# Block 1's attention: probabilities scaled before a transposition by the identity, and the gate product of branch 2 taken out of the eighth head

## The chip, the cores and the metric

The kernel runs on one core of one Trainium2 chip. The metric is the device time of one execution in microseconds (us); the kernel before took 2315.72 us, the median of 3 runs (2314.38 to 2320.10).

## What is computed

Two transformer blocks on 512 tokens of width 1024, in fp32. The first has two branches that read the same normalised input `h`: softmax attention (8 query heads, 2 key/value heads, head size 128) and a bidirectional gated delta rule (8 heads, chunks of 64). Each is gated per head, projected, gated again by a sigmoid of a product with `h`, and added. The change touches the attention of this block and the gate of the second branch:

```python
def block(qi):                                   # 128 queries of one head, 512 keys
    s = jnp.einsum('bkgqd,bksd->bkgqs', qi, k).astype(jnp.float32) * scale
    pr = jax.nn.softmax(s, axis=-1).astype(v.dtype)
    return jnp.einsum('bkgqs,bksd->bkgqd', pr, v)
...
y_att = (o_att * jax.nn.silu(az)) @ w_br_att[i]
y_dn = (o_dn * jax.nn.silu(dz)) @ w_br_dn[i]
mix = (jax.nn.sigmoid(gate_att) * y_att + jax.nn.sigmoid(gate_dn) * y_dn) @ w_out[i]
```

The second block (two layers: stick-breaking attention and differential attention, each with a SwiGLU feed-forward part) is not touched.

## The kernel before

**Matrix products.** Activations are feature-major, 8 tiles of 128 features by 512 tokens. Every large product is made in three matmuls of rounded halves: high weights by high input, high weights by low input, low weights by high input. The weights come as a stream of 1 MB loads (`raw<-wstream`, L1478), each with 16 blocks of 128x128; ACT rounds them to the high half (`w_hi`, L2442), DVE subtracts to get the low half (`w_lo`, L1989). In the profile such matmuls are `ps<-hh,spl` and `ps<-hl,spl` (moving operand first, then the weights). `gemm(op, K, done)` makes one output tile of 128 features: 8 blocks, 24 matmuls, in one of two PSUM banks; `done` starts what evicts it.

**The order** is made before the program is written. `arrange` walks through the large products on PE, and beside them keeps lanes, each a generator of the steps of one side chain: `att_lane` for a head's attention, `conv_lane`, `prep_lane` and `scan_lane` for the delta rule, `silu_lane` and `early_lane` for gates. Between matmuls a lane is advanced when its costs say that its engines are free (`Order.step`, `PRIORITY`, costs in us in `cost=[...]`), or by force when the main stream needs what it holds (`until`). Every engine then runs its own steps in the order of this one list and waits for semaphores; nothing is reordered on the chip. So a changed cost of one step moves others on all engines.

**A head** (loop over `hd`, L695 on) is five large products (convolution inputs k, q and v, attention's query, attention's gate `az`), and from the second head on two more: `dz` of the head before (the delta rule's output gate) and a gate product of branch 2, `early_done(hd - 1)`. `EARLY = 7` says how many of the eight gate products of branch 2 are made among the heads. Such a product is turned into a sigmoid in three steps on ACT (`eg_sig`, tile `X[7]`), stored to HBM by SP (`eg_out`, L1491, printed as `spill<-x`) and loaded again (`eg_ld`, L1498) before the branches are added. After the heads come the eight gate products of branch 1 and the one left of branch 2, and then the products of the attention branch (`ps<-arena_r,spl`). Their operand is what the heads stored: SP loads it tile by tile (`re_ld`, L1526) after the normalised output of the last head (`on_b`, PE `ps<-on_t,cst`, stored at L1516) is out, ACT rounds it, DVE makes its low half (`re_lo`, L2220).

**Attention of one head** is four blocks of 128 queries. `at_s` is the scores (PE, one fp32 matmul 128x512), its row maximum (DVE, L2072) and the exponential with the row sum (ACT, L2439, tile `att_p` in `x`). `at_n` on DVE takes the reciprocal of the sum (L2078) and makes a diagonal matrix of it (L2080). `at_t` multiplies each 128x128 piece of the unnormalised probabilities by the diagonal on PE (`ps<-diag,x`), which transposes and scales at once, and ACT evicts the result (L2442, `x<-ps`). `at_o` is the product with the values (`ps<-x,arena`).

```python
ts(diag[:, :], C["ident"], ri[:, i:i + 1], None, ALU.mult)          # at_n, L2080
i = mm(psum[u.b][:, c], att_p[:, c], diag[:, :], kb == 0, kb == 3)  # at_t, L1655
def tr(out, in_):                                                   # L1551
    return pe.transpose(out, in_, C["ident"])
```

All matmuls are recorded at L1549 (`mm`) and all transpositions but one at L1552 (`tr`). `tr` is used already for the keys and values of the delta rule (`tr_k`, `tr_v`: `ps<-cst,arena` and `ps<-cst,x`).

Of the kernel before, what the change touches and what calls it, by code (L numbers as in the profile page):

```python
# [10 lines left out]
ALU = mybir.AluOpType  # L11
# [4 lines left out]
KT = 8  # L16
EPS = 1e-6
FFN_HALF = 11
EARLY = 7
LAM_INIT = 0.8 - 0.6 * math.exp(-0.3)  # L20
MAGIC = 12582912.0
TWO_PI = 2.0 * math.pi
# [208 lines left out]
def arrange(o, n_pairs):  # L231
# [41 lines left out]
    def gemm(op, K, done):  # L273

        o.until(main.ready)
        u = main.take()
        ks = range(K) if isinstance(K, int) else K
        for k in ks:
            block(u, op, k, k == ks[0], k == ks[-1])
            if k != ks[-1]:  # L280
                o.step()
        done(u)
        o.step()
# [144 lines left out]
    def att_lane(hd):  # L428
        while ("ar_out", f"q{hd}") not in o.at:
            yield  # L430
        o.behind(o.at["ar_out", f"q{hd}"])
        iq, uo = o.at["ar_out", f"q{hd}"].iq, None
        for qb in range(5):
            hint = "AC DV PE"
            yield hint
            while not ring.ready((qb > 0) + (qb < 4)):
                yield hint
            if qb > 1:
                while not uo and not obank_att.ready():
                    yield hint  # L440
                uo = uo or obank_att.take()
                o.behind(o.at["at_t", hd, qb - 2])
                o.add("at_o", hd, qb - 2, cost=[("PE", 0.9)], u=uo)
            t = max(o.now, o.at["at_n", hd, qb - 1].t) if qb else o.now
            if qb:
                banked("at_t", hd, qb - 1, cost=[("PE", 0.45), ("AC", AC_B)])
                o.now = t
            if qb < 4:
                banked("at_s", hd, qb, cost=[("PE", PE_B), ("DV", DV_B), ("AC", AC_B)]).iq = iq
                yield "DV"  # L450
                o.add("at_n", hd, qb, cost=[("DV", 0.15), ("DV", 0.2)])
        o.behind(o.at["at_t", hd, 3])
        yield "PE"
        o.add("at_o", hd, 3, cost=[("PE", 0.9)], u=uo)
        yield "DV"
        q_slots.give(iq, o.at["at_s", hd, 3])
        while ("az_out", hd) not in o.at:
            yield "DV"
        o.behind(o.at["az_out", hd])
        st = o.add("at_m", hd, cost=[("DV", DV_B)])  # L460
        st.u, st.i = uo, o.at["az_out", hd].i
        ua_outs[st.i] += 1
        st.out_n = ua_outs[st.i]
        obank_att.give(uo)
        ua_slots.give(st.i, st)
# [221 lines left out]
    def early_done(m):  # L687
        def done(u):
            u.t = o.clock["PE"]
            o.spawn("egat", early_lane(m, u))  # L690
        return done

    o.margin = MARGIN_1
    for hd in range(8):
        o.spawn("att", att_lane(hd))  # L695
        o.spawn("prep", prep_lane(hd))
        o.spawn("scan", scan_lane(hd))
        o.until(pads.ready)
        gemm(h, KT, conv_done(8 + hd))
        gemm(h, KT, a_rope(f"q{hd}"))  # L700
        o.until(pads.ready)
        gemm(h, KT, conv_done(hd))
        o.until(ua_slots.ready)
        gemm(h, KT, z_done("az", hd, ua_slots))
        o.until(pads.ready)
        gemm(h, KT, conv_done(16 + hd))
        if hd:
            o.until(lambda: not dz_slots.held[(hd - 1) % 2])
            gemm(h, KT, z_done("dz", hd - 1, dz_slots))
            gemm(h, KT, early_done(hd - 1))  # L710
        if hd == 7:
            o.until(lambda: not dz_slots.held[1])
            gemm(h, KT, z_done("dz", 7, dz_slots))
# [561 lines left out]
def build(nc, wstream, wba, consts, vecs, cossin, pos, xT, pT, outT):  # L1275
# [6 lines left out]
    with ctx:  # L1282
# [20 lines left out]
        pad = sb("pad", [128, 2, S])  # L1303
        small = sb("small", [128, 600])
        GS = sb("GS", [128, 2, S])
        diag = sb("diag", [128, 128])
        ident_r = sb("ident_r", [128, 128], F32R)
        mask_r = sb("mask_r", [128, 130], F32R)
        NA = 41
# [235 lines left out]
        def tensor(pe):  # L1545
# [9 lines left out]
            for q in steps:  # L1555
# [92 lines left out]
                elif kind == "at_t":  # L1648
# [3 lines left out]
                    w.wait_ge(sem("at_p"), at[("at_n",) + q.key].n)  # L1652
                    for kb in range(4):
                        c = slice(kb * 128, kb * 128 + 128)
                        i = mm(psum[u.b][:, c], att_p[:, c], diag[:, :], kb == 0, kb == 3)  # L1655
                    i.then_inc(filled[u.b], 1)
                elif kind == "at_o":
                    (hd, qb), u, g = q.key, q.u, q.key[0] // 4
# [308 lines left out]
        def vector(dve):  # L1967
# [15 lines left out]
            for q in steps:  # L1983
# [90 lines left out]
                elif kind == "at_n":  # L2074
# [2 lines left out]
                    empty(s.u)  # L2077
                    dve.reciprocal(ri[:, i:i + 1], sm[:, i:i + 1]).then_inc(sem("at_rcp"), 1)  # L2078
                    w.wait_ge(sem("at_rcp"), q.n)
                    ts(diag[:, :], C["ident"], ri[:, i:i + 1], None, ALU.mult).then_inc(sem("at_p"), 1)  # L2080
                elif kind in ("az_out", "dz_out"):
                    dst = (ua if kind == "az_out" else dz_of)[q.i]
                    w.wait_ge(sem(kind[:2] + "_sig"), 3 * q.n)
# [843 lines left out]
def lay_out(a):  # L2927

    out = []
    blocks = []  # L2930

    def fm(w, c0, n=1, k0=0, k1=None):
        k1 = w.shape[0] // 128 if k1 is None else k1
        for m in range(n):
            for k in range(k0, k1):
                blocks.append(w[k * 128:k * 128 + 128, c0 + m * 128:c0 + m * 128 + 128])
                if len(blocks) == 16:
                    out.append(np.concatenate(blocks, axis=1))
                    blocks.clear()

    def fm2(w, c0, w1, c1):
        for k in range(8):
            fm(w, c0, 1, k, k + 1)
            fm(w1, c1, 1, k, k + 1)

    def tm(w, c0, n):
        assert not blocks
        for j in range(n):
            out.append(w[:, c0 + j * 256:c0 + j * 256 + 256].reshape(8, 128, 256).transpose(1, 0, 2).reshape(128, 2048))

    w = a["w_in"][0]
    fm2(w, 1024, w, 1152)
    tm(w, 1280, 1)
    for hd in range(8):
        fm(w, 2560 + 1024 + 128 * hd)
        fm(w, 128 * hd)
        fm(w, 2560 + 128 * hd)
        fm(w, 1536 + 128 * hd)
        fm(w, 2560 + 2048 + 128 * hd)
        if hd:  # L2960
            fm(w, 5664 + 128 * (hd - 1))
            fm(w, 7712 + 128 * (hd - 1))
    fm(w, 5664 + 128 * 7)
    fm(w, 6688, 8)
    fm(w, 7712 + 128 * EARLY, 8 - EARLY)
    fm(a["w_br_att"][0], 0, 8)
    fm(a["w_br_dn"][0], 0, 8)
    fm(a["w_out"][0], 0, 8)
    fm(a["w_ple_proj"][0], 0, 8)
    fm2(a["w_ple_gate"][0], 0, a["w_ple_gate"][0], 128)  # L2970
    fm(a["w_ple_gate"][0], 256, 6)
    for i in range(2):
        w = a["w_in_2"][i]
        for m in range(8):
            if m == 0 and i == 0:
                fm2(w, 0, w, 1024)
            else:
                fm(w, 128 * m)
                fm(w, 1024 + 128 * m)
            if m == 0:  # L2980
                tm(w, 2048, 4)
        for k0, k1 in ((0, 4), (4, 8)):
            fm(a["w_out_2"][i], 0, 8, k0, k1)
        for half in range(2):
            for k in range(FFN_HALF * half, FFN_HALF * half + FFN_HALF):
                fm(a["w_gate_2"][i], 128 * k)
                fm(a["w_up_2"][i], 128 * k)
            for m in range(8):
                fm(a["w_down_2"][i], 128 * m, 1, FFN_HALF * half, FFN_HALF * half + FFN_HALF)
    assert not blocks  # L2990
    return np.stack(out)
# [55 lines left out]
```

## Time and profile before

| | |
|---|---|
| median of 3 runs | 2315.72 us |
| the profiled execution | 2313.51 us |
| its span, first to last instruction | 2311.7 us |
| granted clock of TensorE, mean | 0.987 of full speed |
| PE busy | 2215.5 us (96%), 15014 matmuls |
| DVE busy | 1185.2 us (51%), 2101 instructions |
| ACT busy | 1011.8 us (44%), 1919 instructions |
| POOL busy | 248.7 us (11%), 273 instructions |
| DMA | 186.31 MB, mean 81 GB/s |

Busy times of the engines overlap; the share of one engine says how far it could be the bound over the whole span, and a stretch has to be looked at by itself. The heads run from about 85 to 640 us, their last side chains and the gate products to about 732 us. A row with an arrow (`<-`) gives the idle time of the engine ahead of the instruction and what ended it.

### The profile page before, as it was taken

The page shows a single profiled execution, that of the slowest core. Times are in us where ns is not written, and L with a number is a line of the kernel's source. Part 1 is how long each engine was busy: PE and PEld are TensorE (multiplying, and loading weights), DVE is VectorE, ACT ScalarE, POOL GpSimd, SP SyncE. Part 2 cuts the span into 40 slices and gives each one's busy share as a digit, 9 for nine tenths or more (in the row PEclk, how much of TensorE's full clock was granted, in tenths as well). Part 3 has the DMA queues.
Part 4 walks back from the last instruction along what each step waited for, and adds up shares of the span by engine and source line. Part 5 has one row for each costly group of instructions (what it writes and reads, how often), then busy time and mean ns, then how long its engine had stood idle before and what let it go on. Part 6 is the DMA issues. An engine that isn't in the chain of part 4 may idle for free.

```text
span 2311.7 us, 35566 instructions
## 1 busy us (share of the span) xinstructions
PE 2215.5 (96%) x15014; PEld 1709.8 (74%) x15014; DVE 1185.2 (51%) x2101; ACT 1011.8 (44%) x1919; POOL 248.7 (11%) x273
## 2 busy tenths in 40 slices
PE   6999999999999999899999999999999988999999
PEld 4777776777776887686656888888886556888887
DVE  5566666565654455523235643454547665443542
ACT  4565655655555235534454322233435544231331
POOL 0022211221220011002221000001001001000000
PEclk9999999999999999999999999999999989999999
DMA  4222211212213432121102232222221112322222
GB/s 168 74 74 74 70 65 57 84 65 66 74 66 116 153 128 91 56 74 40 52 19 78 91 103 98 91 91 99 84 74 37 37 37 73 104 97 91 91 101 81
DMA packets 35054, 186.31 MB, mean 81 GB/s; under 512 B 4032, under 2 KB 4416, under 8 KB 15696
## 3 DMA queue, kind: packets, MB, share of 16 engines
q1 hardware_dynamic: 34896, 184.05, 23.1%
q8 instruction: 118, 1.93, 0.3%
q14 instruction: 40, 0.33, 0.0%
HBM read 173.26 MB, written 8.16 MB: 78 GB/s over the span
## 4 chain that ended last, share of the span: by engine, by line
PE 86%; DVE 7%; ACT 3%; issue 2%; DMA 1%; POOL 0%; SPq 0%; POOLq 0%; DVEq 0%; ACTq 0%
PE ps L1549 85%; ACT arena L2439 1%; DVE spl L1989 1%; PE ps L1552 1%; DVE x L2316 0%; DVE arena L2139 0%; DVE hl L2284 0%; ACT hh L2439 0%; ACT arena L2442 0%; DMA x<-xT 0%; DVE arena L2178 0%; ACT spl L2442 0%; ACT x L2439 0%; DVE x L2280 0%; DVE x L2264 0%
## 5 line engine op out<-in xcount | busy, mean ns | idle before, releaser
L1549 PE MATMUL ps<-hh,spl 128*128 128x512 f32 x3232 | 1067.2, 404 | 31.5 <-DVE arena_r L2216 7.7
L1549 PEld LDWEIGHTS ps<-hh,spl 128*128 128x128 f32 x3232 | 606.1, 189 | 189.8 <-issue 45.2
L1549 PE MATMUL ps<-hl,spl 128*128 128x512 f32 x1552 | 630.9, 407 | 0.0
L1989 DVE TENSOR_TENSOR spl<-raw,spl 128x512 fp32r<-128x512 f32 x596 | 413.6, 720 | 174.0 <-ACT spl L2442 173.0
L1549 PE MATMUL ps<-arena_r,spl 128*128 128x512 f32 x1936 | 474.9, 401 | 9.1 <-DVE arena_r L2216 4.6
L1549 PEld LDWEIGHTS ps<-arena_r,spl 128*128 128x128 f32 x1936 | 366.6, 190 | 105.3 <-DVE arena_r L2216 5.9
L2442 ACT ACTIVATE spl<-raw 128x512 fp32r<-128x512 f32 x596 | 342.4, 618 | 142.2 <-PE ps L1549 141.1
L1549 PEld LDWEIGHTS ps<-hl,spl 128*128 128x128 f32 x1552 | 293.3, 189 | 73.9 <-issue 18.4
L1549 PE MATMUL ps<-arena 32*32 32x32 f32 (+7 forms) x5664 | 217.5, 225 | 16.7 <-issue 6.1
L2439 ACT ACTIVATE arena<-arena 128x512 f32<-128x512 f32 (+3 forms) x209 | 138.4, 663 | 190.3 <-DVE arena L2321 141.5
L1549 PEld LDWEIGHTS ps<-arena 32*32 32x32 f32 (+4 forms) x5664 | 126.2, 116 | 103.1 <-issue 77.1
L1549 PE MATMUL ps<-arena,cst 128*128 128x512 f32 (+3 forms) x308 | 110.2, 483 | 18.6 <-DVE arena L1996 14.3
L2442 ACT ACTIVATE arena_r<-arena 128x512 fp32r<-128x512 f32 x60 | 37.8, 631 | 201.4 <-DVE arena L2328 191.7
L2439 ACT ACTIVATE arena<-ps,small 128x512 f32<-128x512 f32 (+3 forms) x121 | 68.9, 572 | 128.6 <-PE ps L1549 73.5
L2439 ACT ACTIVATE arena<-ps 128x512 f32<-128x512 f32 (+3 forms) x91 | 60.4, 670 | 143.7 <-PE ps L1549 139.6
L2316 DVE TENSOR_TENSOR x<-x,ps 128x512 f32<-128x512 f32 x64 | 43.8, 684 | 147.0 <-PE ps L1549 147.0
L2864 POOL TENSOR_TENSOR arena<-arena 128x512 f32<-128x512 f32 x30 | 38.9, 1296 | 660.0 <-ACT arena L2439 660.0
L1549 PE MATMUL ps<-spl,hh 128*128 128x256 f32 x576 | 108.7, 290 | 0.0
L1549 PEld LDWEIGHTS ps<-spl,hh 128*128 128x128 f32 x576 | 89.9, 191 | 5.5 <-issue 4.9
L1549 PEld LDWEIGHTS ps<-arena,cst 128*128 128x128 f32 x308 | 53.8, 195 | 41.0 <-issue 24.8
L2325 DVE TENSOR_TENSOR arena<-ps,arena 128x512 f32<-128x512 f32 x44 | 30.4, 691 | 104.4 <-PE ps L1549 104.4
L1549 PE MATMUL ps<-spl,hl 128*128 128x256 f32 x288 | 81.3, 282 | 0.0
(218 smaller groups left out, 1927.6 us busy)
## 6 DMA issues: line engine op xcount, KB each, us to landing
raw<-wstream SPq DMA_DIRECT2D x149, 1024.0 KB, 4.9
GS<-g_rows SPq DMA_DIRECT2D x16, 256.0 KB, 3.5
spill<-x SPq DMA_DIRECT2D x15, 256.0 KB, 2.0
arena<-spill SPq DMA_DIRECT2D x13, 256.0 KB, 5.2
arena<-arena SPq DMA_DIRECT2D x20, 128.0 KB, 2.1
on_t<-spill SPq DMA_DIRECT2D x10, 256.0 KB, 3.2
x<-xT SPq DMA_DIRECT2D x4, 512.0 KB, 7.1
spill<-arena SPq DMA_DIRECT2D x8, 256.0 KB, 2.0
```

What stands on the lines that cost most here:

```text
L1549: return pe.matmul(out, lhsT, rhs, start=start, stop=stop, skip_group_check=True)
L1552: return pe.transpose(out, in_, C["ident"])
L1989: tt(spl[:, p % 2, 1, c], raw[:, p % 2, c], spl[:, p % 2, 0, c].bitcast(F32), ALU.subtract) \
L2316: tt(X[q.m], X[q.m], psum[q.u.b][:, :], ALU.add).then_inc(drained[q.u.b], 1)
L2325: tt(p, psum[q.u.b][:, :], SQ[q.g.name][2], ALU.mult).then_inc(drained[q.u.b], 1)
L2439: return act.activation(out, in_, func, **kw)
L2442: return act.activation(out, in_, ACT.Copy)
L2864: tt(acc, acc, tmp[q.i], ALU.add).then_inc(sem("sq_pool"), 1)
```

## The change

In `at_n` DVE multiplies the tile of probabilities itself (128x512, in place) by the column of reciprocals, where it made the 128x128 diagonal; the tile `diag` is gone. `at_t` is four transpositions by the constant identity, through `tr`. The second cost of `at_n` in the planner is 0.5 where it was 0.2. `EARLY` is 6: the second to the seventh head have a gate product of branch 2 each, the eighth none, and product 6 is made with product 7 after the gate products of branch 1, where its sigmoid goes straight to its tile. The weight stream is laid out in the new order.

```diff
--- before.py
+++ after.py
@@ -16,7 +16,7 @@
 KT = 8
 EPS = 1e-6
 FFN_HALF = 11
-EARLY = 7
+EARLY = 6
 LAM_INIT = 0.8 - 0.6 * math.exp(-0.3)
 MAGIC = 12582912.0
 TWO_PI = 2.0 * math.pi
@@ -448,7 +448,7 @@
             if qb < 4:
                 banked("at_s", hd, qb, cost=[("PE", PE_B), ("DV", DV_B), ("AC", AC_B)]).iq = iq
                 yield "DV"
-                o.add("at_n", hd, qb, cost=[("DV", 0.15), ("DV", 0.2)])
+                o.add("at_n", hd, qb, cost=[("DV", 0.15), ("DV", 0.5)])
         o.behind(o.at["at_t", hd, 3])
         yield "PE"
         o.add("at_o", hd, 3, cost=[("PE", 0.9)], u=uo)
@@ -707,7 +707,8 @@
         if hd:
             o.until(lambda: not dz_slots.held[(hd - 1) % 2])
             gemm(h, KT, z_done("dz", hd - 1, dz_slots))
-            gemm(h, KT, early_done(hd - 1))
+            if hd <= EARLY:
+                gemm(h, KT, early_done(hd - 1))
         if hd == 7:
             o.until(lambda: not dz_slots.held[1])
             gemm(h, KT, z_done("dz", 7, dz_slots))
@@ -1303,7 +1304,6 @@
         pad = sb("pad", [128, 2, S])
         small = sb("small", [128, 600])
         GS = sb("GS", [128, 2, S])
-        diag = sb("diag", [128, 128])
         ident_r = sb("ident_r", [128, 128], F32R)
         mask_r = sb("mask_r", [128, 130], F32R)
         NA = 41
@@ -1652,7 +1652,7 @@
                     w.wait_ge(sem("at_p"), at[("at_n",) + q.key].n)
                     for kb in range(4):
                         c = slice(kb * 128, kb * 128 + 128)
-                        i = mm(psum[u.b][:, c], att_p[:, c], diag[:, :], kb == 0, kb == 3)
+                        i = tr(psum[u.b][:, c], att_p[:, c])
                     i.then_inc(filled[u.b], 1)
                 elif kind == "at_o":
                     (hd, qb), u, g = q.key, q.u, q.key[0] // 4
@@ -2077,7 +2077,7 @@
                     empty(s.u)
                     dve.reciprocal(ri[:, i:i + 1], sm[:, i:i + 1]).then_inc(sem("at_rcp"), 1)
                     w.wait_ge(sem("at_rcp"), q.n)
-                    ts(diag[:, :], C["ident"], ri[:, i:i + 1], None, ALU.mult).then_inc(sem("at_p"), 1)
+                    ts(att_p, att_p, ri[:, i:i + 1], None, ALU.mult).then_inc(sem("at_p"), 1)
                 elif kind in ("az_out", "dz_out"):
                     dst = (ua if kind == "az_out" else dz_of)[q.i]
                     w.wait_ge(sem(kind[:2] + "_sig"), 3 * q.n)
@@ -2959,6 +2959,7 @@
         fm(w, 2560 + 2048 + 128 * hd)
         if hd:
             fm(w, 5664 + 128 * (hd - 1))
+        if 0 < hd <= EARLY:
             fm(w, 7712 + 128 * (hd - 1))
     fm(w, 5664 + 128 * 7)
     fm(w, 6688, 8)
```

The changed costs and the missing product move steps on every engine; the order differs from the first attention head to the start of the attention branch, and on PE not after it.

PE, in the first attention head, from its first scores on (`ps<-arena 128x512` is a block's scores, `ps<-cst,arena` a transposition of the delta rule's keys), before:

```order
L1549 MATMUL ps<-arena 128x512
L1549 MATMUL ps<-hl,spl 128x512
L1549 MATMUL ps<-hh,spl 128x512 x2
L1549 MATMUL ps<-hl,spl 128x512
L1549 MATMUL ps<-hh,spl 128x512 x2
L1549 MATMUL ps<-hl,spl 128x512
L1552 MATMUL ps<-cst,arena 128x128 x4
L1549 MATMUL ps<-hh,spl 128x512 x2
L1549 MATMUL ps<-diag,x 128x128 x4
L1549 MATMUL ps<-arena 128x512
```

and with the change:

```order
L1549 MATMUL ps<-arena 128x512
L1549 MATMUL ps<-hl,spl 128x512
L1549 MATMUL ps<-hh,spl 128x512 x2
L1549 MATMUL ps<-hl,spl 128x512
L1549 MATMUL ps<-hh,spl 128x512 x2
L1549 MATMUL ps<-hl,spl 128x512
L1552 MATMUL ps<-cst,arena 128x128 x4
L1549 MATMUL ps<-hh,spl 128x512 x2
L1552 MATMUL ps<-cst,x 128x128 x4
L1549 MATMUL ps<-arena 128x512
```

The first block stands where it stood, with the transpositions in the place of the products; later ones move by some matmuls to either side.

SP, from the rotation transfer of the eighth head's query (L1487) to the first reloads of the attention branch (`arena<-spill`, `on_t<-spill`, L1526; L1482 stores a head's attention, L1516 its delta rule output), before:

```order
L1487 DMA arena<-arena 64x512
L1478 DMA raw<-wstream 128x2048 x3
L1491 DMA spill<-x 128x512
L1482 DMA spill<-x 128x512
L1478 DMA raw<-wstream 128x2048
L1516 DMA spill<-arena 128x512
L1478 DMA raw<-wstream 128x2048 x3
L1516 DMA spill<-arena 128x512
L1526 DMA arena<-spill 128x512
L1526 DMA on_t<-spill 128x512
L1478 DMA raw<-wstream 128x2048
L1526 DMA on_t<-spill 128x512
```

and with the change:

```order
L1487 DMA arena<-arena 64x512
L1478 DMA raw<-wstream 128x2048 x3
L1482 DMA spill<-x 128x512
L1478 DMA raw<-wstream 128x2048
L1516 DMA spill<-arena 128x512
L1478 DMA raw<-wstream 128x2048 x3
L1516 DMA spill<-arena 128x512
L1526 DMA arena<-spill 128x512
L1478 DMA raw<-wstream 128x2048
L1526 DMA on_t<-spill 128x512 x2
```

The gate product's store (L1491) is gone from the eighth head, and a weight load now stands ahead of the second reload, where it stood ahead of the third. On PE, 45 large matmuls stand between the second matmul row of the last `ps<-on_t,cst` and the first `ps<-arena_r,spl`, where there were 48.

## Rows read from the trace of the kernel before

**Rows 1.** The page: busy time of PE, and the granted clock in 40 slices

```profile
PE 2215.5 (96%) x15014; PEld 1709.8 (74%) x15014; DVE 1185.2 (51%) x2101; ACT 1011.8 (44%) x1919; POOL 248.7 (11%) x273
...
PEclk9999999999999999999999999999999989999999
```

**Rows 2.** Windows: busy us of PE, PEld, DVE, ACT, POOL; clock, DMA share, GB/s

```profile
225.00:640.00 415.00, 399.69 (x5499) 308.25 (x5485) 261.63 (x548) 244.19 (x494) 83.60 (x94) 1.00 0.21 70
sum 650.00, PE 622.36 PEld 481.94 DVE 392.38 ACT 377.25 POOL 128.78; mean PE 207.45 PEld 160.65 DVE 130.79 ACT 125.75 POOL 42.93
...
221.00:226.00 5.00, 4.77 (x74) 3.50 (x75) 4.28 (x9) 3.54 (x8) 1.36 (x2) 0.66 0.13 20
735.00:745.00 10.00, 8.38 (x22) 5.64 (x23) 5.99 (x10) 7.22 (x14) 0.00 (x0) 0.66 0.53 159
```

**Rows 3.** Waits of PE, 85 to 740 us: us in total, times, longest

```profile
PE ps L1549 <- issue: 6.1, 6, 1.5
PE ps L1549 <- DVE arena L2178: 5.1, 7, 1.2
PE ps L1549 <- ACT pad L2442: 3.8, 2, 2.9
PE ps L1549 <- DVE arena_r L2220: 3.0, 2, 2.2
PE ps L1549 <- DVE spl L1989: 2.7, 2, 1.5
```

**Rows 4.** Timeline, first attention block: start, us, engine, line, operation

```profile
87.23 0.69 DVE L2072 TENSOR_REDUCE small<-ps 128x1 f32<-128x512 f32 x1 [2.43 <-PE ps L1549]
...
88.77 0.16 DVE L2078 RECIPROCAL small<-small 128x1 f32<-128x1 f32 x1 [0.25 <-ACT x L2439]
88.97 0.29 DVE L2080 TENSOR_SCALAR diag<-cst,small 128x128 f32<-128x128 f32 x1
...
89.60 1.05 PE L1549 MATMUL ps<-diag,x 128*128 128x128 f32 x8
...
90.49 1.02 PE L1549 MATMUL ps<-arena 128*128 128x512 f32 x2
90.69 0.60 ACT L2442 ACTIVATE x<-ps 128x512 f32<-128x512 f32 x1 [0.24 <-PE ps L1549]
```

**Rows 5.** Timeline of PE, a block of transpositions in the eighth head

```profile
646.97 0.60 PE L1552 MATMUL ps<-cst,x 128*128 128x128 f32 x4
647.41 0.61 PE L1549 MATMUL ps<-rv,kdt 128*128 128x128 f32 x4
```

**Rows 6.** Transpositions (L1552), 85 to 735 us: ns min/median/max, first and last start

```profile
L1552 PE MATMUL ps<-cst,arena x48: 270/273/328, 88.7 to 614.0; 128*128 128x128 f32 x48
...
L1552 PE MATMUL ps<-cst,x x16: 270/272/301, 257.2 to 647.3; 128*128 128x128 f32 x16
```

**Rows 7.** Groups of DVE by form (busy, mean ns, idle before), and its longest wait

```profile
L2080 DVE TENSOR_SCALAR diag<-cst,small 128x128 f32<-128x128 f32 x32 | 9.6, 301 | 1.1
...
L2418 DVE TENSOR_SCALAR arena<-arena,small 128x512 f32<-128x512 f32 x8 | 3.9, 487 | 0.3
...
DVE small L2072 <- PE ps L1549: 72.2, 31, 4.9
```

**Rows 8.** Timeline of PE at its longest stop in the heads

```profile
221.23 0.64 PE L1549 MATMUL ps<-hh,spl 128*128 128x512 f32 x1 [2.90 <-ACT pad L2442]
```

**Rows 9.** Timeline of PE in the eighth head

```profile
635.05 0.50 PE L1549 MATMUL ps<-hh,spl 128*128 128x512 f32 x1 [0.69 <-ACT x L2439]
```

**Rows 10.** Timeline of SP's queue and of PE at the attention branch's start

```profile
726.68 0.43 SPq L1526 DMA_DIRECT2D on_t<-spill  x1
...
728.73 0.33 SPq L1478 DMA_DIRECT2D raw<-wstream  x1
729.10 0.43 SPq L1526 DMA_DIRECT2D on_t<-spill  x1
...
735.87 0.96 PE L1549 MATMUL ps<-arena_r,spl 128*128 128x512 f32 x3 [2.21 <-DVE arena_r L2220]
```

## The prediction

> **What bounds the kernel now.** I read the page's busy times first [rows 1]: the matrix engine is at work for 2215.5 of 2311.7 us (96%), VectorE for 1185.2 (51%), and the row of the granted clock shows full speed nearly everywhere. So the kernel is matrix work laid end to end. Then the windows [rows 2] over the stretch that the change touches, from the first attention head (85 us) to the first product of the attention branch (735 us): of 650 us PE is busy 622.4, VectorE 392.4 and ScalarE 377.3. PE is out of work for about 27.6 us there. Then the waits of PE in that stretch [rows 3]: the five longest rows make 20.7 us in 19 waits, in all corners of the side chains (the level products L2178, a bank L2442, the low halves L2220 and L1989). None names L2080, which feeds the product that is changed: the reader is to see that the attention chain is covered today. What is saved on PE's own time here should shorten the span, as far as no side chain is late in its place.
>
> **The change, part by part.**
>
> *The transposition on PE.* In the row of the old form [rows 4] one block's four products with the diagonal are eight records and run from 89.60 us to the next product's start at 90.49: 0.89 us. A fp32 product of 128 columns takes two records, a transposition one. The trace has four transpositions by the identity in the head loop of the same shape [rows 5]: they start at 646.97, and the next product at 647.41: 0.44 us. The change turns 32 such blocks (8 heads by 4) from the one form into the other: 32 x 0.45 = **-14.4 us**, all of it PE's own time. The shared group of transpositions [rows 6] shows the same duration for all 64 that run in this stretch, median 273 and 272 ns, so the price is not a lucky one. The Trainium skill (TensorE: Matmul & The Clock Gate, Terms) calls its transpose mode four times faster for FP32; by that the block would take 0.22 us and the saving be 21.4 us. The rows show half and not a quarter, so the sum goes by the rows.
>
> *The scaling on DVE.* L2080 wrote 128x128 and takes 0.30 us on average. Its new form, a multiplication by a column in place on 128x512 in SBUF, is in the trace in block 2 (L2418): 0.487 us [rows 7]. That is +0.2 us x 32 = 6.4 us of DVE time. I cost it at nothing: before its row maxima alone DVE waits 72.2 us for PE in this stretch [rows 7]. In the first block the old chain [rows 4] ends at 88.97 + 0.29 = 89.26 us and PE comes to the block at 89.60: 0.34 us to spare against 0.20 more, and the planner counts 0.3 us more for the step, so it leaves more matmuls between. What is queued behind it on DVE are the low halves of the weights (L1989), which PE waited for only twice. If this cover is gone, it costs 6.4 us at most.
>
> *What faster PE runs into.* PE's time falls, the chains on ACT and DVE don't. A wait of PE grows by what was saved between the start of the chain it waits for and the wait. From row maximum (87.23) to the end of the eviction of the same block (90.69 + 0.60) is 4.1 us [rows 4], which I take for a chain's length; 19 waits x 4 us are 76 of 650 us or 12% of the stretch, so 12% of 14.4 us are given back: **+1.7 us**. This is an estimate. The ends: below it nothing; a gain too, since the order is planned anew and the longest stop can disappear. That one is 2.90 us at 221.23, where PE waited for a bank whose eviction stood on ACT behind other work [rows 8]; the clock was granted at 0.66 over the 5 us after, which is another 5 x 0.34 = 1.7 us; 4.6 us together. Above it: two such stops more, +9.2 us.
>
> *The product moved out of the eighth head.* The seventh gate product of branch 2, 24 matmuls, is made later, in the tail of gate products, and no matmul is added or dropped: 0 on PE. Its three sigmoid steps on ACT move with it; a store and a load of 256 KB fall away, both off the path. In the eighth head the last product with the head's output gate could start only when the bank of the product that is now gone had been read, by a first sigmoid step that stands on ACT behind others; PE's wait of 0.69 us at 635.05 for such a step [rows 9] should go: **-0.7 us**. Against it stands the start of the branch product. The normalisation of the eighth head now stands 45 instead of 48 main matmuls before it, 3 x 0.23 = +0.7 us. And SP's order (shown with the change) has the 1 MB weight load ahead of the second reload of the attention branch, where it was ahead of the third. That load waits until DVE has finished with the buffer and was issued at 728.73; the second reload went at 726.68 before and must now follow it, as the third did at 729.10, whose product could start at 735.87 only [rows 10]. So the wait that came after six matmuls of `arena_r` comes after three, +0.7 us. Together **+1.4 us**.
>
> After the branch products start, PE's order is the same. **Sum: -14.4 + 1.7 - 0.7 + 1.4 = -12.0 us.** The profiled execution took 2313.5 us (span 2311.7), so it becomes 2301.5. The median of the three runs, 2315.7, lies 2.2 us above that execution; the same step from it gives **2303.7 us**.
>
> **The rivals.** About 0.3%, 6.9 us, is what a measurement of this kernel can tell from no change.
>
> 1. *The cover on DVE is not there.* PE is 2.3% faster in the stretch, and the scaling is late wherever the spare 0.34 us was the rule. Each block then costs its 0.2 us on the path: -12.0 + 6.4 = -5.6 us, 2310.1, within 0.3%. For it speaks the short spare time of the first block, against it that no wait for L2080 is among PE's waits and 72 us of DVE's own waiting. Chance 0.13.
>
> 2. *The clock falls behind the transpositions, and the kernel becomes slower.* 32 blocks that were matmuls are now transpositions. If the clock fell to its lower level (1.2 of 2.4 GHz) after each, a fall of the kind seen in the windows at 221 and 735 us (0.66 over 5 and over 10 us) costs 1.7 us or more: 32 x 1.7 = 54, so -12.0 + 54 = +42 us, 2358. It cancels the gain from the 8th such fall on, and from the 12th ((12.0 + 6.9) / 1.7) the kernel is slower by more than 0.3%. Against it: from 225 to 640 us, with most of the 64 transpositions in it, the granted clock was 1.00 [rows 2, 6], and both falls follow a PE stop of over 2 us. Chance 0.03. The Trainium skill (TensorE: Matmul & The Clock Gate, Part 4: PE-mode transpose) says that transpositions do not count as busy for the clock gate; by that rule this rival would be likelier, and this case's trace does not bear it out for four at a time among full matmuls.
>
> 3. *The new plan has new bank stops.* Order on every engine moves, and a product must start as soon as the last bank is evicted. With two more of the kind of [rows 8]: -12.0 + 9.2 = -2.8, 2312.9. With five more it would be slower (+11). For it: one such stop in eight heads before. Against: DVE and ACT are idle for 40% of the stretch. Chance 0.04, of which 0.01 slower.
>
> 4. *The change doesn't do what it says*: a transposition of this operand costs what the product cost, say because in place of one record it needs two. Then nothing is saved and nothing given back, and only the terms of the moved product stay, -0.7 + 1.4 = +0.7 us, 2316.4. The row of `ps<-cst,x` [rows 6], which reads from the same tile, speaks against it. Chance 0.02.
>
> **How the numbers follow.** The forecast has 0.78 and is faster by over 0.3% in all its own range: -19 (the stop at 221 gone) to -7 us (chains take back 6.5 us and not 1.7). Rivals 1, 4 and most of 3 are within 0.3%: 0.13 + 0.02 + 0.03 = 0.18. Slower are rival 2 and the rest of 3: 0.04. The range reaches from -19 us, 2297, to rival 1 with a microsecond above it, 2311.
>
> **What would show it.** Right: L1552 with `ps<-cst,x` has 144 records (128 more), no `ps<-diag,x`; a block's span about 0.44 us; L2080 at 0.487 us; PE's busy time between 85 and the first `arena_r` product lower by some 14 us; that first product starts 10 to 13 us earlier; its waits for L2220 grow from 3.0 to about 4.4 us; the part after it as long as before. Wrong: a wait of PE for x L2080 of microseconds in total (rival 1); more stretches with a clock under 1 between 85 and 735 us (rival 2); PE's idle time there well above 30 us with `ps` evictions as releasers (rival 3).

## The result, and the profile after

| | before | with the change |
|---|---|---|
| median of 4 runs each | 2316.25 us (2314.38 to 2320.10) | 2302.78 us (2299.77 to 2306.21) |
| the profiled execution | 2313.51 us | 2299.77 us |
| its span | 2311.7 us | 2298.0 us |
| PE busy | 2215.5 us | 2200.8 us |
| DVE busy | 1185.2 us | 1189.3 us |
| ACT busy | 1011.8 us | 1011.5 us |

The ratio is 0.994, with a 95% interval of 0.992 to 0.996: 13.5 us less by the medians, 13.7 by the two profiled spans. The forecast was 12.0 less.

The page of the changed kernel, its busy times and its granted clock, which answer to [rows 1]:

```profile
PE 2200.8 (96%) x14886; PEld 1696.2 (74%) x14886; DVE 1189.3 (52%) x2101; ACT 1011.5 (44%) x1919; POOL 247.9 (11%) x273
...
PEclk9999999999999999999999999999999989999999
```

PE lost 128 matmul records, one of two for each of 128 pieces, and 14.7 us of busy time; 13.7 us of it reached the span.

The timeline of the first attention block, columns as in [rows 4]:

```profile
87.15 0.69 DVE L2072 TENSOR_REDUCE small<-ps 128x1 f32<-128x512 f32 x1 [2.42 <-PE ps L1549]
...
88.68 0.16 DVE L2078 RECIPROCAL small<-small 128x1 f32<-128x1 f32 x1 [0.25 <-ACT x L2439]
88.88 0.49 DVE L2080 TENSOR_SCALAR x<-x,small 128x512 f32<-128x512 f32 x1
...
89.52 0.63 PE L1552 MATMUL ps<-cst,x 128*128 128x128 f32 x4
...
89.98 1.02 PE L1549 MATMUL ps<-arena 128*128 128x512 f32 x2
```

From the block's start to the next product's it is 89.98 - 89.52 = 0.46 us where it was 0.89. The scaling takes 0.49 us where the diagonal took 0.29, ends at 89.37, and PE comes at 89.52 without a wait. The groups by line (L1552, all of the kernel; L2080 by form) are below. `ps<-cst,x` has 132 records and not the 144 of the prediction, since 12 of the delta rule's transpositions now read another buffer (`ps<-cst,arena` has 140 for 128); together they are the 128 more.

```profile
L1552 PE MATMUL ps<-cst,x x132: 270/273/298, 89.5 to 624.2; 128*128 128x128 f32 x132
...
L2080 DVE TENSOR_SCALAR x<-x,small 128x512 f32<-128x512 f32 x32 | 16.2, 505 | 1.1
```

The windows from the first head to the start of the attention branch, before (whose first such product starts at 732.10 us) and after:

```profile
85.00:732.00 647.00, 620.70 (x7811) 480.94 (x7810) 392.38 (x818) 376.12 (x756) 128.78 (x143) 1.00 0.20 70
```

```profile
85.00:717.00 632.00, 605.11 (x7683) 467.30 (x7682) 395.29 (x817) 375.27 (x755) 128.19 (x143) 1.00 0.21 71
...
217.00:222.00 5.00, 4.83 (x136) 3.71 (x137) 3.50 (x7) 4.58 (x9) 1.96 (x2) 0.66 0.16 23
```

PE was out of work for 26.3 us of this stretch before and for 26.9 us after: 0.6 us of the saved time came back as idle time. The one fall of the clock in the heads is still there, 3 us earlier. The waits of PE from 85 to 730 us after, as in [rows 3] (this window also takes in the start of the attention branch):

```profile
PE ps L1549 <- DVE arena L2178: 6.5, 7, 1.2
PE ps L1549 <- issue: 4.1, 8, 1.1
PE ps L1549 <- DVE arena_r L2220: 3.5, 2, 3.0
PE ps L1549 <- ACT arena L2439: 3.1, 4, 1.1
PE ps L1549 <- DVE arena L2035: 2.9, 1, 2.9
PE ps L1549 <- ACT pad L2439: 2.0, 1, 2.0
PE ps L1549 <- ACT pad L2442: 2.0, 1, 2.0
...
PE ps L1549 <- DVE spl L1989: 1.3, 1, 1.3
```

None is for L2080. The long stop at 221 us became shorter (2.9 to 2.0 us), and others grew or are new: 2.9 us behind the rotated query (L2035, 0.8 before), 2.0 for another eviction. At the start of the attention branch, the timelines of SP's queue and of PE:

```profile
711.74 0.33 SPq L1526 DMA_DIRECT2D arena<-spill  x1
713.47 0.33 SPq L1478 DMA_DIRECT2D raw<-wstream  x1
713.85 0.91 SPq L1526 DMA_DIRECT2D on_t<-spill  x2
```

```profile
716.84 0.86 PE L1549 MATMUL ps<-arena_r,spl 128*128 128x512 f32 x3
720.67 6.75 PE L1549 MATMUL ps<-arena_r,spl 128*128 128x512 f32 x15 [2.97 <-DVE arena_r L2220]
```

The first product starts 15.3 us earlier (716.84 for 732.10); the second reload now goes behind the weight load, and PE stops after three matmuls of `arena_r` for 2.97 us, where it stopped after six for 2.21; a second stop is 0.5 us where it was 0.7 [rows 10]. From this product to the end it is 1581.2 us, 1.6 more than before (1579.6), of which the two stops are 0.5; the 13 traces have 1579.2 to 1582.1 us for this part, so the rest is within their spread.

### The profile page after: what moved, and what is told of

Read it like the earlier page. It is cut to its first block, busy times and chain, and to the rows that moved or that the text cites. A ratio compares the mean times of both kernels' runs of the same rounds, so it can differ in the third digit from the quotient of the medians.

```text
span 2298.0 us, 35314 instructions
## 1 busy us (share of the span) xinstructions
PE 2200.8 (96%) x14886; PEld 1696.2 (74%) x14886; DVE 1189.3 (52%) x2101; ACT 1011.5 (44%) x1919; POOL 247.9 (11%) x273
## 4 chain that ended last, share of the span: by engine, by line
PE 86%; DVE 7%; ACT 3%; issue 2%; DMA 1%; POOL 0%; SPq 0%; POOLq 0%; DVEq 0%; ACTq 0%
PE ps L1549 85%; PE ps L1552 1%; ACT arena L2439 1%; DVE spl L1989 1%; DMA on_t<-spill 0%; DMA arena<-arena 0%; DMA raw<-wstream 0%; DVE x L2316 0%; DVE arena L2139 0%; DVE x L2095 0%; ACT spl L2442 0%; ACT arena L2442 0%; ACT hh L2439 0%; DVE arena L2178 0%; DVE hl L2284 0%
## 5 line engine op out<-in xcount | busy, mean ns | idle before, releaser
L2439 ACT ACTIVATE arena<-arena 128x512 f32<-128x512 f32 (+3 forms) x211 | 139.7, 663 | 190.7 <-DVE arena L2321 141.5
L2439 ACT ACTIVATE arena<-ps,small 128x512 f32<-128x512 f32 (+3 forms) x121 | 68.8, 571 | 126.6 <-PE ps L1549 71.5
L2439 ACT ACTIVATE arena<-ps 128x512 f32<-128x512 f32 (+3 forms) x92 | 60.9, 668 | 143.5 <-PE ps L1549 139.3
```

The lines of the kernel that those rows point to most:

```text
L2439: return act.activation(out, in_, func, **kw)
```

## The experiments

Each kernel was timed in turns with the kernel before on the same chip. All differences "to before" below are medians to the median of before of the same call, with the interval of the ratio; the changed kernel stands at -13.5 us (0.992 to 0.996). Where two kernels with the change in them are compared, it is by these differences, and a microsecond or two between them is noise. A gap of 3 us, as between same_order and the changed kernel, is not clear of it either: their intervals overlap.

| kernel | time, us | to before, us | ratio, 95% |
|---|---|---|---|
| same_order | 2306.89 | -10.2 | 0.9938 to 0.9962 |
| ident_product | 2316.90 | -0.2 | 0.9989 to 1.0007 |
| seven_gates | 2302.69 | -14.4 | 0.9925 to 0.9951 |
| gate_move_only | 2317.47 | +0.4 | 0.9995 to 1.0012 |
| scale_twice | 2301.21 | -14.9 | 0.9919 to 0.9949 |
| transpose_twice | 2321.12 | +5.0 | 1.0007 to 1.0025 |
| reloads_first | 2303.59 | -12.6 | 0.9927 to 0.9957 |
| late_copies | 2301.56 | -14.6 | 0.9921 to 0.9958 |
| plan_035 | 2308.95 | -8.0 | 0.9943 to 0.9969 |
| plan_08 | 2309.34 | -7.6 | 0.9954 to 0.9979 |
| true_cost_before | 2316.80 | -0.2 | 0.9989 to 1.0007 |

**same_order: the two instructions alone, every engine in its old order.**

```diff
-ts(diag[:, :], C["ident"], ri[:, i:i + 1], None, ALU.mult).then_inc(sem("at_p"), 1)
+ts(att_p, att_p, ri[:, i:i + 1], None, ALU.mult).then_inc(sem("at_p"), 1)
...
-i = mm(psum[u.b][:, c], att_p[:, c], diag[:, :], kb == 0, kb == 3)
+i = tr(psum[u.b][:, c], att_p[:, c])
```

> The kernel before with only the two instructions exchanged (scaling of the 128x512 tile on DVE, transpositions by the identity on PE); planner costs and seven gate products as before, so every engine keeps its order. Theory (the gain is PE's own time, 32 x 0.45 us, less what the side chains take back): 12 to 14.5 us under before, first product of the attention branch 13 to 15 us earlier than 732.1 us. Rival (the new order, planned with the right cost, makes a good part of the gain): at most 9 us under before, with PE waiting for L2080 or for the chains behind it. Rival (clock falls behind transpositions): more than one stretch under full clock between 85 and 730 us.

Measured 10.2 us under before, between the two. Its waits of PE are those of before, row by row, with small additions:

```profile
PE ps L1548 <- issue: 6.6, 6, 2.1
PE ps L1548 <- DVE arena L2177: 5.1, 7, 1.2
PE ps L1548 <- ACT pad L2441: 4.5, 2, 2.9
PE ps L1548 <- DVE arena_r L2219: 4.3, 4, 3.0
PE ps L1548 <- DVE spl L1988: 2.7, 2, 1.6
```

(lines are one lower, as a line is gone). The additions are 0.5, 0.7 and 1.3 us. Its first product of the attention branch starts at 722.6 us, 9.5 earlier than in before; but the clock fell three times in its heads (at 157, 222 and 366 us), where it fell once in the execution of before. Such a fall costs 1.7 us (0.66 over 5 us, [rows 2]), two more are 3.4. Without them it would be 12.9 us by this estimate. The window:

```profile
85.00:723.00 638.00, 610.29 (x7686) 468.33 (x7685) 400.43 (x819) 376.12 (x757) 129.72 (x143) 0.99 0.21 71
```

PE is out of work for 27.7 us, 1.4 more than before. The heads begin at slightly different times in the traces, so PE's busy time is best counted from the first scores of each trace to its first branch product (before, then same_order, then the changed kernel):

```profile
86.17:732.10 645.93, 619.63 (x7807) 480.40 (x7806) 392.38 (x818) 375.86 (x756) 128.78 (x143) 1.00 0.20 69
```

```profile
86.53:722.62 636.09, 608.38 (x7680) 467.08 (x7678) 400.27 (x818) 375.67 (x756) 129.72 (x143) 0.99 0.21 70
```

```profile
86.09:716.84 630.75, 603.86 (x7679) 466.58 (x7678) 395.29 (x817) 375.00 (x755) 128.19 (x143) 1.00 0.21 70
```

With the two more falls (3.4 us) taken out, same_order's PE time is 14.7 us below before. So the exchange of instructions gives 14.7 us less 1.4 us that the chains take back, less what falls of the clock happen to cost. The changed kernel, with one fall as before, is 15.8 us below: the last 1.1 us of PE's time come with the new order. With the extra falls taken out in the same way, seven_gates, scale_twice, plan_035 and plan_08 are 15.6 to 15.9 us below, too.

**ident_product: the scaling of the change, but four plain products by the identity.**

```diff
-i = mm(psum[u.b][:, c], att_p[:, c], diag[:, :], kb == 0, kb == 3)
+i = mm(psum[u.b][:, c], att_p[:, c], C["ident"], kb == 0, kb == 3)
```

> As same_order, but the block is four plain products with the identity instead of transpositions: PE's work is that of before, DVE's scaling that of the change (+0.2 us x 32 = 6.4 us of DVE time). Theory (DVE's time is covered): within 1.5 us of before. Rival (each block's 0.2 us lies on the path): 4 to 6.4 us over before.

0.2 us under before: DVE's 6.4 us more are not on the path, and in the old order all of the gain is the transposition's form.

**scale_twice: a second multiplication, by 1.0, behind the first.**

```diff
-ts(att_p, att_p, ri[:, i:i + 1], None, ALU.mult).then_inc(sem("at_p"), 1)
+ts(att_p, att_p, ri[:, i:i + 1], None, ALU.mult).then_inc(sem("at_sc"), 1)
+w.wait_ge(sem("at_sc"), q.n)
+ts(att_p, att_p, 1.0, None, ALU.mult).then_inc(sem("at_p"), 1)
```

> The changed kernel with a second multiplication (by 1.0) of the same tile on DVE behind the first: about 0.5 us more from the row sum to the transposition in each of 32 blocks, 16 us of DVE time. Theory (most blocks have spare time ahead of the transposition; the first one has 0.15 us): PE waits for L2080's successor in some blocks, 0.35 us each, 1 to 5 us over the changed kernel. Rival (DVE's chain sets the pace of the heads and the first scaling was paid already): 10 us or more over it.

It costs nothing that can be measured (1.4 us under the changed kernel), less than the theory allowed. DVE does 14.2 us more, and of all 32 blocks one made PE wait, the first (the waits of PE, then the group):

```profile
PE ps L1552 <- DVE x L2082: 0.3, 1, 0.3
...
L2082 DVE TENSOR_SCALAR x<-x 128x512 f32<-128x512 f32 x32 | 14.2, 444 | 1.1
```

The spare time of the first block, from which I argued, is the shortest of all; the others have more.

**transpose_twice: each block transposed twice into the same bank.**

```diff
-for kb in range(4):
-    c = slice(kb * 128, kb * 128 + 128)
+for kb in range(8):
+    c = slice(kb % 4 * 128, kb % 4 * 128 + 128)
     i = tr(psum[u.b][:, c], att_p[:, c])
```

> The changed kernel with every block's four transpositions made twice into the same bank: 128 more transpositions, nothing else. Theory (PE's own time at 0.11 us each, with no effect on the clock): 11 to 14 us over the changed kernel, that is back to before within 3 us; granted clock between 85 and 730 us not lower than in the other runs (one to four falls of 3.4 us). Rival (transpositions let the clock fall): more than ten such falls in the heads and 25 us or more over the changed kernel.

18.5 us over the changed kernel, above the 11 to 14 of the theory and below the 25 of the rival. In the two traces the busy time of PE from the first scores to the first branch product is 621.6 for 603.9 us, 17.7 more:

```profile
87.81:737.39 649.58, 621.57 (x7808) 483.30 (x7806) 395.16 (x817) 375.48 (x755) 128.07 (x143) 0.99 0.20 68
```

32 x 0.44 = 14.1 us of it are the transpositions; the clock fell three times in these heads (at 286, 402 and 453 us), two falls more than in the trace of the change, which is 3.4 us. Together they are 17.5 of the 17.7. Idle time is 28.0 for 26.9. But kernels with fewer transpositions had as many falls: same_order and seven_gates three, and gate_move_only, where no block of attention is transposed by the identity, four. Besides one at 222 us its windows show them as a mean granted clock of 0.76 and less:

```profile
368.00:375.00 7.00, 6.43 (x156) 4.06 (x160) 3.71 (x7) 3.71 (x7) 2.22 (x2) 0.76 0.35 140
405.00:415.00 10.00, 9.68 (x64) 7.54 (x65) 4.93 (x11) 3.57 (x8) 0.89 (x2) 0.66 0.35 117
641.00:646.00 5.00, 4.53 (x40) 4.13 (x35) 1.92 (x3) 0.86 (x2) 0.00 (x0) 0.66 0.02 3
```

So the falls don't follow transpositions; a rival of one fall per block or of ten in all is out. Whether 256 transpositions bring one or two more in the mean can't be told from single traces. The mean granted clock of its ten executions is 0.9847, where the other three kernels of the same call with the change in them have 0.9852 to 0.9860: 1 to 3 us of 2319, the size of one or two falls. But plan_08, with 128 transpositions, has 0.9844 over five executions, so an order alone can do as much.

**seven_gates and gate_move_only: the attention's part without the moved product, and the moved product alone.** The edits are `EARLY = 7` in the changed kernel and `EARLY = 6`, with the two conditions that read it, in the kernel before.

> The changed kernel with EARLY = 7: the attention's part of the change with its new planner cost, and the gate product left in the eighth head. Theory (the moved product is worth +0.7 us at most either way): within 1.5 us of the changed kernel. Rival (taking the product out of the eighth head is worth something, 3 us or more): 3 us or more over the changed kernel, with PE waiting for a bank in the eighth head.

> The kernel before with EARLY = 6 alone. Theory: -0.7 us for the bank wait in the eighth head, +1.4 us at the start of the attention branch if SP's order there is the changed one: between -1 and +1.5 us of before. Rival (the moved product gives part of the gain): 3 us or more under before.

-14.4 us to before and +0.4: the first is as fast as the changed kernel (0.9 us under it), the second as slow as before. The moved product is worth nothing that can be measured.

The traces show more. The new order at the start of the attention branch does not come with the moved product: seven_gates, which leaves the product in the eighth head, has it (45 large matmuls behind the last normalisation, the weight load ahead of the second reload, a stop of 3.19 us after three matmuls), and gate_move_only does not (49 large matmuls, the load ahead of the third reload, 2.30 us after six). PE at that place in gate_move_only, then in seven_gates:

```profile
743.62 0.96 PE L1550 MATMUL ps<-arena_r,spl 128*128 128x512 f32 x3 [2.30 <-DVE arena_r L2221]
```

```profile
724.00 0.96 PE L1549 MATMUL ps<-arena_r,spl 128*128 128x512 f32 x3 [3.19 <-DVE arena_r L2220]
```

It comes with the attention's new plan.

**reloads_first: SP issues the second and third reload ahead of the weight load.**

```diff
+if q.n in (2, 3):
+    continue
 src = (spill if which == "ya" else spill2)[:, k, :]
 sp.dma_start(stage_of[q.i], src).then_inc(sem(f"re_ld{q.i}"), 16)
+if q.n == 1:
+    for k in (1, 2):
+        i = at["re_ld", "ya", k].i
+        sp.dma_start(stage_of[i], spill[:, k, :]).then_inc(sem(f"re_ld{i}"), 16)
```

> The changed kernel, where SP issues the second and third reload of the attention branch right behind the first, ahead of the weight load. Theory (the weight load's place in SP's order sets the stop at the start of the attention branch, 2.97 us): that stop shrinks to 1 us or less, the time by 1 to 3 us. Rival (the reloads' own time on the DMA engines sets it): the stop stays at 2.5 to 3 us, the time the same.

The time is that of the changed kernel within noise (+0.9). The long stop went from the second tile to the fourth, with a shorter one at the third, and the sum of the stops did not shrink (the timelines of PE, SP's queue and ACT at that place):

```profile
723.65 1.56 PE L1555 MATMUL ps<-arena_r,spl 128*128 128x512 f32 x6
726.41 0.97 PE L1555 MATMUL ps<-arena_r,spl 128*128 128x512 f32 x3 [1.19 <-DVE arena_r L2226]
729.89 1.51 PE L1555 MATMUL ps<-arena_r,spl 128*128 128x512 f32 x3 [2.51 <-DVE arena_r L2226]
```

```profile
718.88 0.91 SPq L1532 DMA_DIRECT2D on_t<-spill  x2
720.28 0.33 SPq L1478 DMA_DIRECT2D raw<-wstream  x1
722.37 0.63 ACT L2448 ACTIVATE arena_r<-on_t 128x512 fp32r<-128x512 f32 x1 [0.23 <-DMA on_t<-spill]
722.89 0.32 SPq L1528 DMA_DIRECT2D arena<-spill  x1
728.48 0.63 ACT L2448 ACTIVATE arena_r<-arena 128x512 fp32r<-128x512 f32 x1 [2.33 <-DMA arena<-spill]
```

The second reload, now ahead of the load, was there 3.5 us after its issue (722.37 - 718.88); the fourth, the first one behind it, after 5.6 us (728.48 - 722.89). The other traces agree: at this place, in all 13, the reloads ahead of the 1 MB load landed 2.6 to 3.9 us after their issue and the first one behind it 5.3 to 6.1. So the rival holds in its result, a stop of 2.5 us and the same time: SP's order decides which tile is late and after how many matmuls PE stops, and some reload is always behind the load.

**late_copies: the four ACT copies behind the level matrices as a step of their own.**

```diff
-st = add("pr_kk", hd, cost=[("PE", 1.7), ("DV", 2 * DV_B), ("DV", 8 * DV_S), ("AC", 1.2)], hold=True)
+kk = st = add("pr_kk", hd, cost=[("PE", 1.7), ("DV", 2 * DV_B), ("DV", 8 * DV_S)], hold=True)
...
+yield "AC"
+add("pr_c", hd, cost=[("AC", 1.2)], ring_=False).u = kk.u
...
-elif kind == "pr_kk":
+elif kind == "pr_c":
```

> The changed kernel, where the four ACT copies of each head's pr_kk are a step of their own, put behind on ACT once DVE is through, so that ACT does not stand before them waiting; the plan is made anew. Theory (a bank's eviction behind those copies makes the stops of 2 to 3 us in the heads, and stops are what the clock falls after): the stop near 217 us goes, the heads are 3 to 6 us shorter. Rival (ACT's standing there is covered, as it is idle 40% of the heads anyway): within 2 us of the changed kernel.

1.1 us under the changed kernel, inside both spreads, as the rival had it. The stop near 217 us is gone and its fall of the clock too, but others came: this trace has one fall as well, at 378 us, and PE's idle time is 634.0 - 605.05 = 29.0 us for 26.9.

```profile
85.00:719.00 634.00, 605.05 (x7686) 467.24 (x7685) 404.66 (x822) 376.53 (x759) 132.70 (x143) 1.00 0.21 72
```

**plan_035, plan_08 and true_cost_before: only the planner's costs.** The first two have 0.35 and 0.8 for 0.5 as the cost of the scaling in the changed kernel. The third sets the PE cost of `at_t` in the kernel before to 0.89 for 0.45.

> The changed kernel with 0.35 in place of 0.5 as the planner's cost of the scaling, so only the order differs. same_order (the old order) was 10 us under before, the order of the changed kernel 14 under. Theory (an order in itself is worth a few us either way, by which stops and falls of the clock it meets, and the stated cost is no better for being true): between 2 us under and 4 us over the changed kernel. Rival (the true cost makes the better plan): 2 to 4 us over the changed kernel, as far as same_order.

> The changed kernel with 0.8 as the planner's cost of the scaling. Theory (orders differ by chance): between 2 us under and 4 us over the changed kernel. Rival (the true cost is the best): 2 us or more over.

> The kernel before, with the planner's cost of a block's product with the diagonal set to the 0.89 us that it takes, where the plan has 0.45: same instructions, another order. Rival (the old plan was poor because it took the block for half as long as it is, and the change is faster partly since its plan is true): 2 us or more under before. Theory (orders differ by chance): within 3 us of before either way.

The first two are 5.5 and 5.9 us over the changed kernel, more than the 4 us that the theory allowed for either, and their instructions are the same. For plan_08 the rival (2 us or more over) holds; plan_035 is outside its rival's 2 to 4 us as well. The third is at before (-0.2). The waits of PE of plan_08, from 85 to 740 us, show what an order can bring:

```profile
PE ps L1549 <- DVE spl L1989: 5.4, 3, 3.2
PE ps L1549 <- DVE arena_r L2220: 4.3, 4, 2.9
PE ps L1549 <- ACT pad L2442: 4.0, 1, 4.0
...
PE ps L1549 <- ACT x L2442: 3.2, 1, 3.2
```

Three stops of over 3 us in the heads, the one of 4.0 us for an eviction of a convolution's bank as at 221 us before, where the changed kernel has none over 2.9; and three falls of the clock for one. The true cost was the best of the four values tried (0.2 in same_order, 0.35, 0.5, 0.8), which is in favour of the rival; but a true cost for PE in the kernel before brought nothing, and same_order with 0.2 is better than 0.35. Whether a truer plan is better, or this one had luck, stays open.

## Why the prediction was right

*The transposition, -14.4 us.* Right: the blocks went from 0.89 to 0.44 us (0.46 in the first), same_order's PE time fell by 14.7, ident_product shows that nothing else in the exchange counts, and transpose_twice has the price a second time in its trace. The half of the rows held, not the quarter that the prediction worked out from the Trainium skill (TensorE: Matmul & The Clock Gate, Terms).

*The scaling costs nothing.* Right, with more cover than I saw: scale_twice laid another 14.2 us on DVE and PE waited 0.3 us in all. Rival 1 falls.

*What faster PE runs into, +1.7 us.* In the old order it is +1.4 us of idle time (same_order). In the changed kernel it was +0.6, and PE's busy time from the first scores on fell by 15.8 us where the exchange explains 14.7; so the first branch product came 15.3 us earlier, not the 10 to 13 that I had given. The last 1.1 us is in all the traces with the new plan and not in same_order, so it comes with the order; which instructions gain it stays open. The 12% of the stretch, from a chain's length and the number of waits, came near for the old order alone.

*The moved product, -0.7 + 1.4 us.* Here the sum has parts that were wrong, and the total came out near for all that. The bank wait did go: no wait of PE for an ACT step on `x` of L2439 is left in the list of waits. The +1.4 was booked under the wrong cause: seven_gates shows that the new order at the branch's start comes with the attention's plan. Of its two parts one is seen. The stop after three matmuls instead of six is 2.97 us for 2.21, the +0.7 that I had read from the rows; in both traces the late tile's first matmul starts 3.8 us after the first branch product. The other +0.7, for 45 matmuls instead of 48, did not add to it: the normalisation does stand closer (the first reload is issued 5.1 us before the first branch product, where it was 5.8), but the weight load, behind which the late tile lands, is issued 3.4 us before that product in both traces (728.73 to 732.10, 713.47 to 716.84). The two stops grew by 0.5 us together (3.0 to 3.5), not by 1.4. In the time none of it is visible (gate_move_only +0.4 us, seven_gates 0.9 under the changed kernel).

*The clock, rival 2.* The falls don't come behind the blocks. In the traces with the transpositions the last block of attention ended 10 us or more before each fall in the heads; the one exception, in late_copies at 378 us, falls in a block, but 1.4 us behind a stop of PE of 2.1 us. The rule that the prediction took from the Trainium skill (TensorE: Matmul & The Clock Gate, Part 4: PE-mode transpose), that transpositions do not count as busy for the clock gate, is not borne out by blocks of 0.44 us among full matmuls, nor clearly by blocks twice as long; no run here has a long stretch of transpositions alone.

*Bank stops, rival 3.* It did not come in the changed kernel, but it is real: plan_08 is this rival, with the changed kernel's own instructions, at about half of its gain. I had given it 0.04 from a count of one such stop in the old order, which was too little. Three other orders of the changed attention (same_order, plan_035, plan_08) were 3.3, 5.5 and 5.9 us over the changed kernel, and two (seven_gates, late_copies) about 1 us under it, so the gain is 8 to 15 us by order. The sum was right for the order at hand with some luck: its terms other than the first are smaller than what an order makes of them. The traces add up as -14.7 (the exchange), -1.1 (PE's time in the new order), +0.6 (idle time in the heads) and +1.6 us (from the first branch product on), in all -13.6.

## What to carry to other kernels

Where PE is the bound and a product with a diagonal matrix only transposes and scales, scale on an engine with time to spare and transpose by the identity: in fp32 a block of four cost 0.44 instead of 0.89 us. Read the price from a transposition of the same shape that the kernel already has. In a kernel whose order is made by a planner, time the edit once in the old order and once in the new; here the difference was 3 us (not clear of noise), and with other cost values up to 6. Let each kernel's trace say which change an order came with: here a new order of loads was put down to the moved product and belonged to the other half of the change.

## What the runs showed of the hardware

The executions of one kernel that take longer mostly have the lower mean clock. The four executions of the changed kernel had spans and mean granted clocks of 2298.0 (0.987), 2299.6 (0.986), 2302.2 (0.984) and 2304.4 us (0.984): 0.003 of 2300 us is 6.9 us, the spread is 6.4. A fall to the lower level (1.2 GHz) costs 1.7 us or a multiple of it: with that taken out for each, PE's time in the heads agrees within 0.3 us between traces with one, two and three falls (scale_twice, plan_035, seven_gates). The traces have up to four in the heads, and where one kernel has them another with the same order has none: same_order has two (157 and 366 us) that before has not.

All 26 falls in the heads of the 13 traces began while PE stood still or up to 2.3 us after it had, 24 of them at a stop of 1.2 to 4.0 us and two at one of 0.7 us. The reverse does not hold: stops of 2.90 us (at 134 us in the changed kernel) and 3.18 us (at 295 us in plan_08) brought no fall. Which stops bring one is not settled by these traces.

At the start of the attention branch a 256 KB reload landed 2.6 to 3.9 us after its issue when it was ahead of a 1 MB load in SP's queue and 5.3 to 6.1 us when it was the first one behind it.

So two single traces of kernels a few us apart are compared by idle time and by falls first, and by span last, and each from the same instruction on: a window from 85 us on had 1.7 us more of what lies ahead of the heads in transpose_twice than in the changed kernel.
